# A hybrid decoder step (Conformer convolution and mLSTM) on one core: the head loop's norm, tile sums, state output and the place of the weight splits reordered

## The chip, the cores and the metric

The kernel runs on one core of one Trainium2 chip. The metric is the time of one execution on the device, in microseconds (us). A core has TensorE (PE in the rows, with its weight load as PEld), VectorE (DVE), ScalarE (ACT), GpSimd (POOL) and SyncE (SP). They run side by side and wait for each other through semaphores.

## The reference

One trunk layer runs over 512 prompt tokens and over 8 decode sequences of 4 tokens. Cut to what matters here, the mLSTM branch, for each of 4 heads with DK = 256 and DV = 512:

```python
s = jnp.einsum('bthk,bshk->btsh', qc, kc) * w_intra
num = jnp.einsum('btsh,bshv->bthv', s, vc) + w_inter[..., None] * jnp.einsum('bhvk,bthk->bthv', C, qc)
den = jnp.sum(s, axis=2) + w_inter * jnp.einsum('bhk,bthk->bth', n, qc)
h = num / jnp.maximum(jnp.abs(den), jnp.exp(-m_t))[..., None]
C_new = dec[..., None, None] * C + jnp.einsum('bsh,bshv,bshk->bhvk', wk, vc, kc)
n_new = dec[..., None] * n + jnp.einsum('bsh,bshk->bhk', wk, kc)
...
hm = hm * lax.rsqrt(jnp.mean(hm * hm, axis=-1, keepdims=True) + EPS) * g_mh.reshape(M_HEADS, DV)
hm = hm.reshape(B, T, D_M).astype(x.dtype) * jax.nn.sigmoid(o)
y_m = jnp.einsum('btm,md->btd', hm, w_m_out)
```

With N = num and d = max(|den|, exp(-m)), N/d normed is N / sqrt(mean(N^2) + EPS d^2). Around this branch stand the input projection, a 31-tap depthwise convolution, gates, an output projection and a two-matrix MLP. All tensors are float32.

## The kernel before

Every weight is streamed from memory in chunks of 128 output features (512 KB). SyncE loads a chunk into one of two buffers `wraw`, ScalarE copies it as rounded float into `whi` (a ring of 4), VectorE writes the rest `wlo = wraw - whi`, and TensorE makes each product from three partial ones (whi with ahi, whi with alo, wlo with ahi). The function `hi` issues the ScalarE part, `lo` the VectorE part; inside the head loop both are called by `split(k)`, where k counts the head's 12 chunks: 0 to 3 are q and k, 4 to 7 are v, 8 to 11 are the output gates o0 to o3. `split(12)`, `split(13)` and `split(14)` already belong to the next head's q0, q1 and k0. SyncE refills a `wraw` buffer when the `lo` of it is done.

The order of the work is written out by hand for each engine, and an engine takes its list in that order. The head loop (`with pe.Fori(0, HEADS)` and the same on the others) is run 4 times. TensorE has two product buffers in PSUM, slot 0 and slot 1. The table `USES` lists what a head puts into them: an even place is slot 0, an odd one slot 1. TensorE may write a use only when the use before it in the same slot has been drained (`use(name)` waits for `drained`). Its o chunks are in slots 0, 1, 0, 1. Between them it makes the outer products cu0 to cu7 (`outer(n)`, new terms of the decode sequences' matrix memories), each of which is drained by VectorE's `update(n)` of the ring `crg` (L1145). `readout(i)` multiplies four of the old memories with the queries. After o3 come the weighted values pv0 to pv3 (`weighted(k)`), and the prompt's new memory (`new_state(half)`), which uses the slots as cc01 and cc23.

In the o section ScalarE and VectorE run this (before):

```python
# ScalarE                                    # VectorE
split(10)                                    rden = max(rden, exp(-m)); taps(15, 16); split(10)
for k in range(VT):                          for k in range(VT):
    split(11 + k)                                if k != 1: taps(*O_TAPS[k])
    hm_k = sigmoid(product of o_k)               split(11 + k)
                                                 if k == 1: taps(*O_TAPS[k])
                                                 if k < 2: update(2 * k); update(2 * k + 1)
```

`taps(a, b)` (L1035) runs taps a to b-1 of the depthwise convolution, two instructions a tap; they need nothing of the products and are spread over the head as filling. In the pv section VectorE multiplies each pv by the reciprocal `rden` into `hr` (L1168), multiplies the gate `hm` by that (L1171), and adds the squares that ScalarE makes of `hr` into `sqacc` (L1176). A matmul with ones sums them over partitions, and ScalarE makes the root. `den` is a matmul of ones with the four tiles of `pt`; the normaliser sums are eight one-column matmuls over `kw`.

Of the kernel before, what the change touches and what calls it, by code (L numbers as in the profile page):

```python
# [11 lines left out]
P = 128  # L12
# [37 lines left out]
        "cu4", "pv0", "cu5", "pv1", "cc01", "cu6", "pv2", "cu7", "pv3", "cc23"]  # L50
# [42 lines left out]
DVE_PER_HEAD = 81  # L93
# [22 lines left out]
def hybrid_layer(nc, xT, wstream, w_gates, cols, b_gates, b_v, w_dw, hist, c_in, n_in, m_in,  # L116
# [8 lines left out]
    with ctx:  # L125
# [30 lines left out]
        eps = at("eps", [P, 1], f32)  # L156
        warm = at("warm", [P, 1], f32)
# [41 lines left out]
        bv = at("bv", [P, DV], f32, cursor[0])  # L199
        hr = at("hr", [P, 2, SEQ], f32)  # L200
# [98 lines left out]
        np_ready, np_used, nn_ready = sem("np_ready"), sem("np_used"), sem("nn_ready")  # L299
# [102 lines left out]
        def _(pool):  # L402
# [28 lines left out]
            pool.memset(sel[:, :], 0.0).then_inc(pool_step, 1)  # L431
            for j in range(QUAD):
                pool.wait_ge(pool_step, 18 + j)
                pool.affine_select(out=sel[:, :], in_=sel[:, :], compare_op=ALU.not_equal, fill=1.0, base=-NS * j,
                                   pattern=[[-1, NS]], channel_multiplier=1).then_inc(pool_step, 1)
# [52 lines left out]
            def prompt_state(h):  # L488
                for name in ("cc01", "cc23"):
                    wait_drained(pool, h, name)  # L490
# [14 lines left out]
            with pool.Fori(0, HEADS - 1) as h:  # L505
# [8 lines left out]
                pool.wait_ge(head_done, h + 1)  # L514
# [14 lines left out]
        def _(act):  # L529
# [98 lines left out]
            act.wait_ge(pool_step, 22)  # L628
            with act.Fori(0, HEADS) as h:
# [88 lines left out]
                def state_out(half):  # L718
                    s = use(("cc01", "cc23")[half])
                    act.activation(cst[:, 2 * half:2 * half + 2, :].rearrange("p a k -> p (a k)"), psum[s][:, 0, :],  # L720
                                   ACT.Copy).then_inc(drained[s], 1)

                act.wait_ge(np_ready, h + 1)
                act.activation(npn[:, bass.ds(h, 1), :], side[:, 2:3, P:P + QT], ACT.Copy).then_inc(np_used, 1)
                for k in range(VT):
                    was_drained(f"pv{k}")
                    if k == 3:
                        act.wait_ge(hsum_ready, 3 * h + 1)
                    dst = sqacc[:, :] if k == 0 else sqh[:, k % 2, :]
                    act.activation(dst, hr[:, k % 2, :], ACT.Square).then_inc(hsq_ready, 1)  # L730
                    if k == 1:
                        state_out(0)
# [3 lines left out]
                act.activation(sqacc[:, :], side[:, 1, :], ACT.Ln, bias=eps[:, :], scale=1.0 / DV).then_inc(var_ready, 1)  # L736
# [124 lines left out]
        def _(dve):  # L861
# [148 lines left out]
            dve.wait_ge(pool_step, 22)  # L1010
            with dve.Fori(0, HEADS) as h:
# [88 lines left out]
                for s_ in range(ST):  # L1100
# [5 lines left out]
                    if s_ >= 2:  # L1106
                        if s_ == 3:
                            dve.wait_ge(dve_step, sums_at)
                        n = sample_products(s_ - 2)
                    if s_ < 3:  # L1110
# [25 lines left out]
                rd = mark(V.tensor_tensor(rden[:, :], rden[:, :], hb[:, R_M:R_M + SEQ], ALU.max))  # L1136
                dve.wait_ge(sden_abs, h + 1)
                sd = mark(V.tensor_tensor(sst[:, 0:1], sst[:, 0:1], mcol[:, hh], ALU.max))
                taps(15, 16)
# [8 lines left out]
                for k in range(VT):  # L1148
                    if k != 1:
                        taps(*O_TAPS[k])  # L1150
                    split(11 + k)
                    if k == 1:
                        taps(*O_TAPS[k])
# [3 lines left out]
                    if k == 1:  # L1157
                        dve.wait_ge(dve_step, sd)
                        V.reciprocal(sst[:, 1:2], sst[:, 0:1]).then_inc(srec_ready, 1)
                        dve.wait_ge(dve_step, rd)  # L1160
                        rd = mark(V.reciprocal(rden[:, :], rden[:, :]))
                dve.wait_ge(dve_step, rd)
                for k in range(VT):
                    update(4 + k)
                    s = use(f"pv{k}")
                    if k >= 2:
                        dve.wait_ge(hsq_ready, VT * h + (k - 1))
                    V.tensor_tensor(hr[:, k % 2, :], psum[s][:, 0, :], rden[:, :], ALU.mult).then_inc(drained[s], 1)  # L1168
                    was_drained(f"pv{k}")
                    d = tile(hm, 4 * h + k, 0, SEQ)  # L1170
                    n = mark(V.tensor_tensor(d, d, hr[:, k % 2:k % 2 + 1, :], ALU.mult))  # L1171
                    if k >= 1:
                        dve.wait_ge(hsq_ready, VT * h + (k + 1))
                        if k >= 2:
                            dve.wait_ge(hsum_ready, 3 * h + (k - 1))
                        V.tensor_tensor(sqacc[:, :], sqacc[:, :], sqh[:, k % 2, :], ALU.add).then_inc(hsum_ready, 1)  # L1176
                    taps(*PV_TAPS[k])
                taps(26, WIDTH - 1)
# [8 lines left out]
                dve.wait_ge(dve_step, n)  # L1187
# [578 lines left out]
```

## Time and profile before

| | us |
|---|---|
| median of 3 runs (lowest, highest) | 1281.4 (1280.85, 1281.85) |
| profiled execution, its own time | 1282.05 |
| its span in the trace | 1280.4 |
| TensorE busy | 1242.6 |
| VectorE busy | 730.1 |
| ScalarE busy | 494.2 |

The profiled execution's own time is 1.65 us above its span and 0.65 us above the median. TensorE's busy time is the union of its matmuls' times. The mean granted TensorE clock of the span is 0.988 of full speed.

### The profile page before, as it was taken

The numbers are of one execution on the slowest core, as the hardware profiler recorded it, in microseconds if no ns is written. First come the engines' busy times: TensorE is split into PE (matmuls) and PEld (weight loads), VectorE is DVE, ScalarE is ACT, GpSimd is POOL, SyncE is SP. The second block draws the span as 40 slices with busy tenths as digits, with TensorE's granted clock in tenths as the row PEclk, the third lists the DMA queues.
The fourth block names the chain that finished last, engine by engine and source line by source line (L and its number), as shares of the span: only waits on it lengthen the run. The fifth ranks groups of instructions, "written<-read, shape, count | busy, mean of one in ns | idle before, by whom it ended". The sixth has DMA issues, their size and how long they took to land.

```text
span 1280.4 us, 23631 instructions
## 1 busy us (share of the span) xinstructions
PE 1242.6 (97%) x9079; PEld 1164.1 (91%) x9079; DVE 730.1 (57%) x984; ACT 494.2 (39%) x738; POOL 68.6 (5%) x130
## 2 busy tenths in 40 slices
PE   7999999999999999999999999998999999999994
PEld 6999978888797888879999999997999999999993
DVE  6342688888878888888455433337453213443324
ACT  5333543343354335335543222236564223543211
POOL 3010001101100110010000000000000000000002
PEclk8999999999999999999999999998999999999997
DMA  6235216515441641442322222430323222223211
GB/s 205 81 117 186 83 66 214 187 37 186 172 145 41 221 178 62 150 162 84 100 82 99 83 90 78 149 99 34 104 94 99 82 98 82 83 82 99 82 49 70
DMA packets 39328, 141.29 MB, mean 110 GB/s; under 512 B 4788, under 2 KB 5172, under 8 KB 39144
## 3 DMA queue, kind: packets, MB, share of 16 engines
q1 hardware_dynamic: 27848, 99.37, 23.2%
q0 software_dynamic: 11424, 41.23, 9.1%
q8 instruction: 29, 0.48, 0.1%
q14 instruction: 27, 0.22, 0.1%
HBM read 118.31 MB, written 22.26 MB: 110 GB/s over the span
## 4 chain that ended last, share of the span: by engine, by line
PE 91%; DVE 4%; issue 2%; ACT 2%; DMA 1%; DVEq 0%; POOLq 0%; POOL 0%; SPq 0%; ACTq 0%
PE product L1365 85%; PE side L1365 6%; DVE hr L1168 1%; DVE hm L1191 1%; DVE accp L1035 1%; DMA x<-in_xT 1%; DVE y L1279 1%; DVE crg L1145 0%; ACT sqh L730 0%; ACT L700 0%; PE side L1523 0%; DVE qT L1056 0%; ACT rst L551 0%; DVE hm L1184 0%; ACT rst L553 0%
## 5 line engine op out<-in xcount | busy, mean ns | idle before, releaser
L872 DVE TENSOR_TENSOR wlo<-wraw,whi 128x1024 fp32r<-128x1024 f32 x176 | 215.3, 1224 | 234.6 <-ACT whi L535 220.8
L1365 PE MATMUL product<-ahi,whi 128*128 128x256 f32 x1520 | 319.4, 291 | 12.1 <-DVE alo L1289 5.9
L1365 PE MATMUL product<-ahi,wlo 128*128 128x256 f32 x1520 | 315.3, 289 | 0.0
L1365 PE MATMUL product<-alo,whi 128*128 128x256 f32 x1520 | 313.5, 287 | 0.0
L535 ACT ACTIVATE whi<-wraw 128x1024 fp32r<-128x1024 f32 x176 | 184.3, 1052 | 237.1 <-PE product L1365 183.9
L1365 PEld LDWEIGHTS product<-ahi,whi 128*128 128x128 f32 x1520 | 244.9, 190 | 19.6 <-issue 11.9
L1365 PEld LDWEIGHTS product<-alo,whi 128*128 128x128 f32 x1520 | 244.4, 189 | 0.0
L1365 PEld LDWEIGHTS product<-ahi,wlo 128*128 128x128 f32 x1520 | 243.7, 189 | 0.0
L1035 DVE SCALAR_TENSOR_TENSOR accp<-u,wdw,accp 128x512 f32<-128x512 f32 x240 | 162.9, 742 | 0.3
L1365 PE MATMUL product<-hidhi,wlo 128*128 128x256 f32 (+1 forms) x512 | 105.8, 287 | 0.0
L1365 PE MATMUL product<-hidlo,whi 128*128 128x256 f32 (+1 forms) x512 | 105.7, 288 | 0.0
L1365 PE MATMUL product<-hidhi,whi 128*128 128x256 f32 (+1 forms) x512 | 104.8, 286 | 0.0
L1365 PEld LDWEIGHTS product<-hidhi,wlo 128*128 128x128 f32 x512 | 82.0, 188 | 0.0
L1365 PEld LDWEIGHTS product<-hidhi,whi 128*128 128x128 f32 x512 | 81.9, 188 | 0.0
L1365 PEld LDWEIGHTS product<-hidlo,whi 128*128 128x128 f32 x512 | 81.2, 188 | 0.0
L1314 DVE TENSOR_TENSOR hidlo<-fr,hidhi 128x544 f32 (+1 forms) x32 | 23.2, 726 | 74.9 <-ACT hidhi L822 74.9
L1365 PE MATMUL product<-whi,ahi 128*128 128x512 f32 (+1 forms) x160 | 56.4, 352 | 0.0
L1365 PE MATMUL product<-wlo,ahi 128*128 128x512 f32 (+1 forms) x160 | 55.6, 347 | 0.0
L1365 PE MATMUL product<-whi,alo 128*128 128x512 f32 (+1 forms) x160 | 55.4, 346 | 0.0
L1365 PE MATMUL product<-mhi,wlo 128*128 128x256 f32 (+1 forms) x256 | 52.9, 288 | 0.0
L1365 PE MATMUL product<-bhi,wlo 128*128 128x256 f32 (+1 forms) x256 | 52.9, 288 | 0.0
L1365 PE MATMUL product<-mhi,whi 128*128 128x256 f32 (+1 forms) x256 | 52.9, 288 | 0.0
(268 smaller groups left out, 1604.7 us busy)
## 6 DMA issues: line engine op xcount, KB each, us to landing
wraw<-in_wstream SPq DMA_DIRECT2D x176, 512.0 KB, 3.3
crg<-in_c_in POOLq DMA_DIRECT2D x32, 512.0 KB, 5.9
out_c_s<-crg POOLq DMA_DIRECT2D x32, 512.0 KB, 2.9
hb<-head_rows POOLq DMA_DIRECT2D x4, 580.0 KB, 5.5
x<-in_xT SPq DMA_DIRECT2D x4, 544.0 KB, 5.7
sgm<-in_xT SPq DMA_DIRECT2D x1, 2176.0 KB, 9.0
out_yT<-y SPq DMA_DIRECT2D x8, 272.0 KB, 2.1
out_c_p<-cst POOLq DMA_DIRECT2D x4, 512.0 KB, 8.5
```

Source lines behind the costliest of these rows:

```text
L535: act.activation(whi[:, k % RING, :, :], wraw[:, k % 2, :, :], ACT.Copy).then_inc(hi_done, 1)
L872: V.tensor_tensor(wlo[:, k % RING, :, :], wraw[:, k % 2, :, :], whi[:, k % RING, :, :].bitcast(f32), ALU.subtract).then_inc(lo_done, 1)
L1035: ins = V.scalar_tensor_tensor(sum_, src, w, sum_, ALU.mult, ALU.add)
L1168: V.tensor_tensor(hr[:, k % 2, :], psum[s][:, 0, :], rden[:, :], ALU.mult).then_inc(drained[s], 1)
L1191: ins = V.scalar_tensor_tensor(d, d, c("g_mh", 4 * h + k), sqacc[:, :].rearrange("p (a t) -> p a t", a=1), ALU.mult, ALU.mult)
L1279: V.scalar_tensor_tensor(tile(y, j), tile(y, j), c(gain, j), rst3, ALU.mult, ALU.mult).then_inc(y_scaled, 1)
L1314: V.tensor_tensor(tile(hidlo, j), fr[:, 2 + b:3 + b, :], tile(hidhi, j).bitcast(f32), ALU.subtract).then_inc(hid_lo, 1)
L1365: return pe.matmul(out, lhsT, rhs, start=start, stop=stop, skip_group_check=check)
```

## The change

- `USES` loses cc01 and cc23. The new state is made in four quarters in the PSUM tensor `side`, a quarter ahead of each weighted value, the last one in two halves around pv3. ScalarE copies it from there; new semaphores `cc_ready` and `cst_ready` stand for the slots' ones.
- The denominator no longer divides: d squared, scaled, is the first term of `sqacc`, and the norm's root is taken of the whole. The reciprocal of `rden` (L1161) and the products `hr` (L1168) are gone; ScalarE squares pv straight from PSUM and VectorE multiplies the gate by pv.
- VectorE adds the tiles of `pt` into `sqacc` and those of `kw` into the new tile `ksum`, so that the ones-matmuls for the denominator are two instead of four and those for the normaliser two instead of eight.
- `readout(0)` comes ahead of o0 on TensorE, and the one-column matmuls come behind `outer(2)`.
- On ScalarE the load of the sigmoid's table (the `warm` activation) comes ahead of the loop over the o chunks, and in the loop the sigmoid of o_k now comes ahead of `split(11 + k)`. On VectorE `split(11 + k)` comes first for every k, and the taps are dealt out anew. GpSimd's load of the next head's bias no longer waits for `head_done`.

The core of the diff:

```diff
-V_TAPS = [(5, 8), (8, 11), (11, 15)]
-O_TAPS = [(16, 17), (17, 19), (19, 23), (23, 24)]
-PV_TAPS = [(24, 24), (24, 26), (26, 26), (26, 26)]
+V_TAPS = [(5, 8), (8, 11), (11, 14)]
+O_TAPS = [(14, 14), (14, 17), (17, 22), (22, 24)]
+PV_TAPS = [(24, 25), (25, 26), (26, 27), (27, 27)]
...
                 act.activation(rden[:, :], side[:, 0, :], ACT.Abs).then_inc(den_abs, 1)
-                act.wait_ge(sden_ready, h + 1)
-                act.activation(sst[:, 0:1], side[:, 2, 0:1], ACT.Abs).then_inc(sden_abs, 1)
                 split(10)
+                act.wait_ge(d_ready, h + 1)
+                act.activation(sqacc[:, :], rden[:, :], ACT.Square, scale=(EPS * DV / P) ** 0.5).then_inc(hsq_ready, 1)
+                act.activation(warm[:, :], eps[:, :], ACT.Sigmoid).then_inc(table_in, 1)
                 for k in range(VT):
-                    split(11 + k)
-                    if k == 0:
-                        act.activation(warm[:, :], eps[:, :], ACT.Sigmoid).then_inc(table_in, 1)
                     s = use(f"o{k}")
                     act.activation(tile(hm, 4 * h + k), slot(s), ACT.Sigmoid, bias=c("b_o", 4 * h + k)).then_inc(drained[s], 1)
+                    split(11 + k)
+                    if k == 1:
+                        act.wait_ge(sden_ready, h + 1)
+                        act.activation(sst[:, 0:1], side[:, 2, 0:1], ACT.Abs).then_inc(sden_abs, 1)
+                        act.activation(npn[:, bass.ds(h, 1), :], side[:, 2:3, P:P + QT], ACT.Copy).then_inc(np_used, 1)
...
                 for k in range(VT):
-                    if k != 1:
-                        taps(*O_TAPS[k])
                     split(11 + k)
-                    if k == 1:
-                        taps(*O_TAPS[k])
+                    taps(*O_TAPS[k])
                     if k < 2:
                         update(2 * k)
                         update(2 * k + 1)
...
-                    V.tensor_tensor(hr[:, k % 2, :], psum[s][:, 0, :], rden[:, :], ALU.mult).then_inc(drained[s], 1)
-                    was_drained(f"pv{k}")
+                    dve.wait_ge(hsq_ready, (VT + 1) * h + (k + 2))
                     d = tile(hm, 4 * h + k, 0, SEQ)
-                    n = mark(V.tensor_tensor(d, d, hr[:, k % 2:k % 2 + 1, :], ALU.mult))
+                    if k < VT - 1:
+                        V.tensor_tensor(d, d, psum[s][:, 0:1, :], ALU.mult).then_inc(drained[s], 1)
                     if k >= 1:
+                        dve.wait_ge(hsum_ready, VT * h + k)
+                    V.tensor_tensor(sqacc[:, :], sqacc[:, :], sqh[:, k % 2, :], ALU.add).then_inc(hsum_ready, 1)
...
+                pe.wait_ge(wsum_ready, h + 1)
+                mm(side[:, 0, 0:P], ones[:, :], pt[:, 0:P], True, True)
+                mm(side[:, 0, P:SEQ], ones[:, :], sqacc[:, P:SEQ], True, True).then_inc(den_ready, 1)
+                readout(0)
+                chunk("o0", 8)
...
+                for k in range(VT):
+                    outer(4 + k)
+                    if k == VT - 1:
+                        new_state(k, range(2))
+                    elif k > 0:
+                        new_state(k)
+                    weighted(k)
+                new_state(VT - 1, range(2, ST))
```

**The order on ScalarE, around the sigmoid of o1.** `hm` is the gate, product0 and product1 are the slots, `whi` is the `hi` step of a split. Before, from the sigmoid of o0 on:

```order
L702 ACTIVATE hm_73<-product0,col_52 128x544
L532 REGISTER_ALU
L535 ACTIVATE whi_50<-wraw_49 128x1024 [waits chunk_done,raw_in0]
L321 REGISTER_ALU
L702 ISA [waits chunk_done]
L702 REGISTER_ALU
L702 ACTIVATE hm_73<-product1,col_52 128x544
```

Now, from the same place on:

```order
L703 ACTIVATE hm_74<-product0,col_52 128x544
L537 REGISTER_ALU [waits raw_in1]
L538 ACTIVATE whi_50<-wraw_49 128x1024 [waits chunk_done]
L325 REGISTER_ALU
L703 ISA [waits chunk_done]
L703 REGISTER_ALU
L703 ACTIVATE hm_74<-product1,col_52 128x544
L535 REGISTER_ALU
L538 ACTIVATE whi_50<-wraw_49 128x1024 [waits chunk_done,raw_in0]
```

The copy of chunk 12 (the one with raw_in0) stood ahead of o1's sigmoid and its wait for the end of chunk o1 and now stands behind them; between the two sigmoids there is now that of chunk 11.

**The order on VectorE, around update(2).** `crg` is an update of a matrix memory, `wlo` the `lo` step of a split, `accp` a tap. Before, from update(1) on:

```order
L1145 SCALAR_TENSOR_TENSOR crg_116<-crg_116,hb_93,product0 128x1024 [waits ready0]
...
L872 TENSOR_TENSOR wlo_51<-wraw_49,whi_50 128x1024 [waits hi_done]
...
L1035 SCALAR_TENSOR_TENSOR accp_113<-u_82,wdw_53,accp_113 128x512
...
L1145 SCALAR_TENSOR_TENSOR crg_116<-crg_116,hb_93,product0 128x1024 [waits ready0]
L1145 SCALAR_TENSOR_TENSOR crg_116<-crg_116,hb_93,product1 128x1024 [waits ready1]
```

Now:

```order
L1159 SCALAR_TENSOR_TENSOR crg_117<-crg_117,hb_94,product0 128x1024 [waits ready0]
...
L875 TENSOR_TENSOR wlo_51<-wraw_49,whi_50 128x1024 [waits hi_done]
...
L1038 SCALAR_TENSOR_TENSOR accp_114<-u_83,wdw_53,accp_114 128x512
...
L1159 SCALAR_TENSOR_TENSOR crg_117<-crg_117,hb_94,product0 128x1024 [waits ready0]
L1159 SCALAR_TENSOR_TENSOR crg_117<-crg_117,hb_94,product1 128x1024 [waits ready1]
```

The sequence is the same, but the row of the tap stands for 4 instructions before and for 6 now, and the `wlo` is in both that of chunk 12, whose `hi` has moved on ScalarE.

**The order on TensorE, around o2.** `product0<-vst,kst` is the outer product cu2, `product1<-vst,kst` is cu3, and the last row is the first matmul of o2. Now:

```order
L1373 MATMUL product0<-vst_112,kst_111 128x512 [waits drained0]
...
L1373 MATMUL side<-ones_54,ksum_97 128x1 [waits ksum_ready]
...
L1373 MATMUL product1<-vst_112,kst_111 128x512 [waits drained1]
...
L1373 MATMUL product0<-ahi_71,whi_50 128x256 [waits drained0]
```

o2 takes slot 0 behind cu2, as before; between cu2 and cu3 stand now five one-column matmuls (two of `ksum`, one of `pts`, two of `qn`) where eight of `kw` stood.

## Rows read from the trace of the kernel before

**Rows 1.** The page: busy us (share of the span) xinstructions of two engines.

```profile
PE 1242.6 (97%) x9079; PEld 1164.1 (91%) x9079; DVE 730.1 (57%) x984; ACT 494.2 (39%) x738; POOL 68.6 (5%) x130
```

**Rows 2.** Waits of PE over the whole span: us in total, times, longest.

```profile
PE product L1365 <- DVE hr L1168: 2.6, 8, 0.3
...
PE product L1365 <- DVE qT L1056: 2.1, 3, 0.8
```

**Rows 3.** Timeline of PE, third head: start us, us, instruction [idle before <-releaser].

```profile
404.93 2.32 PE L1365 MATMUL side<-pt,ones 128*128 128x512 f32 x8
...
414.12 1.92 PE L1365 MATMUL side<-crg,qm 128*32 128x512 f32 x16
...
417.48 1.12 PE L1365 MATMUL side<-vtok,pts 32*128 32x512 f32 x2
418.53 0.52 PE L1365 MATMUL product<-ahi,whi 128*128 128x256 f32 x2
...
424.63 0.62 PE L1365 MATMUL product<-vst,kst 96*128 96x512 f32 x2
425.10 1.84 PE L1365 MATMUL side<-ones,kw 128*128 128x1 f32 x16
426.80 0.71 PE L1365 MATMUL product<-vst,kst 96*128 96x512 f32 x2
427.35 0.42 PE L1365 MATMUL product<-ahi,whi 128*128 128x256 f32 x2
...
439.42 1.92 PE L1365 MATMUL side<-crg,qm 128*32 128x512 f32 x16
...
443.92 0.70 PE L1365 MATMUL product<-vst,kst 96*128 96x512 f32 x2
...
447.21 3.62 PE L1365 MATMUL product<-kw,vtok 128*128 128x256 f32 x16
...
461.37 1.02 PE L1365 MATMUL side<-sqacc,ones 128*128 128x512 f32 x2
```

**Rows 4.** Timeline of DVE in the same stretch, same columns.

```profile
416.75 2.47 DVE L1145 SCALAR_TENSOR_TENSOR crg<-crg,hb,product 128x1024 f32<-128x1024 f32 x2 [0.34 <-PE product L1365]
419.13 1.22 DVE L872 TENSOR_TENSOR wlo<-wraw,whi 128x1024 fp32r<-128x1024 f32 x1
420.27 2.74 DVE L1035 SCALAR_TENSOR_TENSOR accp<-u,wdw,accp 128x512 f32<-128x512 f32 x4
425.30 1.28 DVE L1145 SCALAR_TENSOR_TENSOR crg<-crg,hb,product 128x1024 f32<-128x1024 f32 x1 [2.29 <-PE product L1365]
...
459.83 6.71 DVE L1035 SCALAR_TENSOR_TENSOR accp<-u,wdw,accp 128x512 f32<-128x512 f32 x10
```

**Rows 5.** Timeline of ACT in the same stretch, same columns.

```profile
413.59 1.06 ACT L535 ACTIVATE whi<-wraw 128x1024 fp32r<-128x1024 f32 x1 [1.55 <-DMA wraw<-in_wstream]
414.67 1.28 ACT L700 ACT_TABLE_LOAD   x1
...
417.31 1.06 ACT L535 ACTIVATE whi<-wraw 128x1024 fp32r<-128x1024 f32 x1 [0.54 <-DMA wraw<-in_wstream]
425.05 0.71 ACT L702 ACTIVATE hm<-product,col 128x544 f32 x1 [6.68 <-PE product L1365]
425.66 1.05 ACT L535 ACTIVATE whi<-wraw 128x1024 fp32r<-128x1024 f32 x1
```

**Rows 6.** Timeline of PE after its longest idle time, in the MLP; same columns.

```profile
873.60 0.79 PE L1365 MATMUL product<-ahi,whi 128*128 128x256 f32 x2 [5.93 <-DVE alo L1289]
...
878.20 0.41 PE L1365 MATMUL product<-alo,whi 128*128 128x256 f32 x2
```

**Rows 7.** Windows there: stretch, length, busy of PE PEld DVE ACT POOL, PEclk, DMA.

```profile
870.00:872.00 2.00, 0.00 (x0) 0.00 (x0) 1.97 (x3) 0.60 (x1) 0.00 (x0) 0.82 0.00 0
...
876.00:878.00 2.00, 2.00 (x10) 2.00 (x10) 1.96 (x4) 1.21 (x3) 0.00 (x0) 0.50 0.00 0
878.00:880.00 2.00, 2.00 (x18) 2.00 (x17) 1.97 (x4) 1.03 (x2) 0.00 (x0) 0.98 0.00 0
```

More of the change, by code:

```diff
@@ L49 @@
         "o0", "cu0", "cu1", "o1", "cu2", "cu3", "o2", "o3",
-        "cu4", "pv0", "cu5", "pv1", "cc01", "cu6", "pv2", "cu7", "pv3", "cc23"]
+        "cu4", "pv0", "cu5", "pv1", "cu6", "pv2", "cu7", "pv3"]
 USES_HEAD = len(USES) // 2
@@ L1135, in _ @@
                 dve.wait_ge(expm_ready, h + 1)
[L1136 to L1139, printed above, removed]
+                V.scalar_tensor_tensor(rden[:, :], hb[:, R_M:R_M + SEQ], D_CAP, rden[:, :], ALU.min, ALU.max).then_inc(d_ready, 1)
                 split(10)
@@ L1565, in weighted, with new_state @@
                     ins.then_inc(ready[s], 1)
-                def new_state(half):
-                    s = use(("cc01", "cc23")[half])
-                    for r in range(2):
-                        for q in range(ST):
-                            v = P * (2 * half + r)
-                            ins = mm(psum[s][:, 0, DK * r:DK * (r + 1)], vtok[:, q, v:v + P], kw[:, q, :], q == 0, q == ST - 1)
-                    ins.then_inc(ready[s], 1)
-                pe.wait_ge(pt_ready, 5 * h + 5)
-                for q in range(ST):
-                    ins = mm(side[:, 0, P * q:SEQ], ones[:, :], pt[:, PT_AT[q]:PT_AT[q] + SEQ - P * q], q == 0, q == ST - 1)
-                ins.then_inc(den_ready, 1)
-                pe.wait_ge(ops_ready, 5 * h + 4)
+                def new_state(v, tiles=range(ST)):
+                    half, r = divmod(v, 2)
+                    for q in tiles:
+                        ins = mm(side[:, half, DK * r:DK * (r + 1)], vtok[:, q, P * v:P * (v + 1)], kw[:, q, :], q == 0, q == ST - 1)
+                    if r == 1 and q == ST - 1:
+                        ins.then_inc(cc_ready, 1)
+                pe.wait_ge(pt_ready, 5 * h + 5)
+                pe.wait_ge(wsum_ready, h + 1)
[3 more added lines that the diff above has]
+                chunk("o0", 8)
+                pe.wait_ge(ops_ready, 5 * h + 5)
+                pe.wait_ge(vs_all, h + 1)
+                pe.wait_ge(kst_ready, 3 * DEC_B * (h + 1))
+                outer(0)
+                mm(side[:, 3, :], pts[:, :], vtok[0:NS, ST, :], False, False)
+                outer(1)
+                chunk("o1", 9)
+                outer(2)
+                pe.wait_ge(ksum_ready, h + 1)
+                for kk in range(QT):
+                    mm(side[:, 2, P + kk:P + kk + 1], ksum[:, P * kk:P * (kk + 1)], ones[:, 0:1], True, True)
                 mm(side[:, 2, 0:1], pts[:, :], ones[0:NS, 0:1], True, False)
@@ L1584, in _ @@
                 ins.then_inc(sden_ready, 1)
-                chunk("o0", 8)
-                readout(0)
-                pe.wait_ge(ops_ready, 5 * h + 5)
-                pe.wait_ge(vs_all, h + 1)
-                pe.wait_ge(kst_ready, 3 * DEC_B * (h + 1))
-                outer(0)
-                outer(1)
-                mm(side[:, 3, :], pts[:, :], vtok[0:NS, ST, :], False, False)
-                chunk("o1", 9)
-                outer(2)
-                pe.wait_ge(sden_abs, h + 1)
-                for kk in range(QT):
-                    for q in range(ST):
-                        ins = mm(side[:, 2, P + kk:P + kk + 1], kw[:, q, P * kk:P * (kk + 1)], ones[:, 0:1], q == 0, q == ST - 1)
-                ins.then_inc(np_ready, 1)
                 outer(3)
```

92 lines of the change are left out of this document (47 added, 45 removed).

## The prediction, made blind

> **What bounds the kernel now.** I read the page first: TensorE is busy for 1242.6 us of the span, VectorE for 730.1 and ScalarE for 494.2 [rows 1]. So the time is TensorE's list plus its gaps, and an edit elsewhere counts when it opens or closes one. The waits of TensorE in the head loop are small: 2.6 us in 8 waits for the products `hr`, and 2.1 us in 3 waits for `qT` at the start of a head [rows 2]. Then I read the timelines of the three engines over one head. The rows to look at are the ones around o1 and o2: VectorE does update(0) 0.34 us after it could, waiting for TensorE, and it stood idle 2.29 us before update(2), for TensorE again [rows 4]. So before, VectorE is ahead of TensorE by about 2 us where o2 needs its slot. ScalarE copies chunk 12 at 417.31, over 7 us ahead of o1's sigmoid at 425.05, and chunk 13 right behind that sigmoid [rows 5]. That lead is what the change touches. All times below are those of the third head; the others have the same list.
>
> **What TensorE saves.** The four ones-matmuls for the denominator take 2.25 us from start to next (the row at 404.93, 8 records for 1280 columns) [rows 3]; two matmuls of 512 columns in all take 512/1280 of it, 0.90: 1.35 us saved. The eight one-column matmuls over `kw` take 1.70 (425.10 to 426.80), two take 0.43: 1.27 saved. Matmuls of the new state are the same in number. Together 2.6 us a head, 10.5 in all. With the waits for `hr` gone (2.6) the best case of the change is 13 us.
>
> **VectorE's added and removed work** counts only through the order. Three additions of `kw` (256 wide) and three of `pt` (384, 256, 128 wide) replace a tap and the reciprocal; the `pt` sums stand behind v3, while TensorE makes v4, and I cost their wait at nothing (the cover is v4's own product; if it were missing, the sums' own length of under 1.5 us a head would be the price, by twice the 0.67 us of a tap [rows 4]).
>
> **Step A, o1.** o0 now starts at 404.93 + 0.90 + 1.9 (the readout's row at 414.12) = 407.7, and ends 6.1 later (418.53 to 424.63) at 413.8. TensorE then has cu0 0.47, the product of `pts` 1.05 and cu1 0.47 [rows 3] and wants o1 at 415.8. o1 needs slot 1, so update(0). VectorE now has `split(11)` ahead of it, and ScalarE has o0's sigmoid ahead of that. A sigmoid starts 0.42 after TensorE's next row (424.63 to 425.05), the copy follows 0.61 later and takes 1.05 [rows 5], the `wlo` takes 1.14, the update 1.28 [rows 4]; with 0.1 for two handovers the slot is free at 413.8 + 4.6 = 418.4. Before, o1 began at 418.53. So TensorE waits 2.6 us, and the 1.35 saved ahead of it and the one-column matmuls that moved away are gone into that wait: gain 0.1.
>
> **Step B, o2.** This is the large one. Counted from the end of o1 (424.5): sigmoid +0.42, copy of chunk 12 +0.61 and 1.05, `wlo` 1.14, six taps at 0.67 = 4.0 (ten take 6.71, four 2.74), update(2) 1.28, handovers 0.1: o2 starts 8.6 us after o1's end, at 433.1. Before it was 427.35 [rows 3], since chunk 12 was split long ago and the taps done. TensorE's own list in between is cu2 0.47, five one-column matmuls 1.2 and cu3 0.55, so it stands still for about 6.4 us. Price: 5.8 us a head.
>
> **Step C, the clock.** Such a pause was in the trace once: 5.93 us idle, in the course of which the granted clock fell (0.82 in one stretch of 2 us, 0.50 afterwards, 0.98 again in the last) [rows 7], that is from 2.4 to 1.2 GHz, and the ten pairs of matmuls behind it took 4.6 us, 873.60 to 878.20 [rows 6], where ten pairs take 2.5 at full clock (a chunk has 48 matmuls, 24 pairs, in its 6.1). I take the same 2.1 us for each of the four pauses; the bounds are 0 and, with the smaller pauses of step A and D also bringing it down, three times that.
>
> **Step D, o3 and the pv section.** o3 follows o2 at once. TensorE's list reaches the point of the old `readout(1)` at 433.1 + 2.1 + 12.07 (427.35 to 439.42) = 447.3. VectorE: o2 ends at 441.3; sigmoid, copy and `wlo` as above bring it to 444.6, ten taps to 451.3, `split(14)` to 452.4, four taps to 455.1, update(4) to 456.4. TensorE would want the slot (cu5) after a quarter of the new state, 1.8 (half of the row at 447.21), and after readout, cu4 and pv0, 4.5 (439.42 to 443.92), at 453.6. A wait of 2.8. From there the list is that of 443.92 to 461.37, 17.45 us, less 1.4 of old waits (three, 0.3 to 0.4 in the row and some 0.15 at the issue) and less the quarter that now lies ahead, 1.8, plus some 0.5 for updates that come just late: 14.8. The matmul for the sum of squares is at 471.2 instead of 461.37: **+9.8 us a head**, of which B is 5.8 (A's gain in it), C 2.1 and D 1.9. For the four heads 39.2.
>
> **Step E, the next head.** k0 waits for `qT`, 0.7 us each time [rows 2]. Before, VectorE's last ten taps end at 459.83 + 6.7 = 466.5, 5.1 after the start of the sum's matmul at 461.37 [rows 3, 4]. Now the last addition ends just ahead of that matmul, and a product (0.67, the length of a tap of the same width) and eight taps (5.4) follow: 6.0. The list behind is the same, so this wait grows by 0.8, three times: 2.4.
>
> Edits that I cost at nothing: the earlier table load (1.28 us [rows 5]; it stands while TensorE is in o0, where ScalarE is idle; cost 1.28 a head if o0 were over), the new squares and copies (the same number as before within one), GpSimd's bias load (no one waits for it in these rows), and the earlier `readout(0)` (its memories are loaded while the q to v chunks run).
>
> **Sum.** 1282.05 (the profiled execution's own time) + 39.2 + 2.4 = 1323.65; less the 0.65 by which that execution lies above the median: **1323.0 us**.
>
> **The rivals.** *The clock holds.* The waits of under 3 us in A and D do nothing to it and the fall behind o2's pause doesn't come: 8.4 less, 1314.6. Against it speaks that an idle time of the same length was followed by 1.2 GHz [rows 6, 7]. *It falls in three places a head.* After 2.6 to 2.8 us of idle time in front of o1 and cu5 as well: up to 2.1 more each, 8 times, 1340; some of that would lie in waits that are there anyway, so between the two. For it speaks that a pause is closely followed by the next. Against it, 0.3 us waits leave no mark in the head loop, and there is no row with a pause of this length.
>
> The Trainium skill, in TensorE: Matmul & The Clock Gate, section "A second HAM failure mode: psum-queue depth-cycling", describes a kernel in which many short idle times between groups of matmuls kept the clock swinging between half and full rate. By that rule the result would be this second rival's. The trace's short waits do not bear it out so far, and the longest one agrees only in what a long pause does.
>
> *The waits do not come and it is faster.* The mechanism: update(2) is done within the 2.2 us that TensorE has between o1 and o2, so the saved matmuls reach the end. Then 2.6 a head and the waits for `hr` come off: 1281.4 - 13 = 1268.4. It decides at a length of 2.2 us for the chain behind o1's sigmoid, and mine is 8.6; only if copy and `wlo` of chunk 12 ran ahead of the sigmoid, which the orders of both engines exclude, or VectorE did not take its list in order, would it be near. For it speaks only that VectorE had 2.29 us to spare at this point. *The change does not do what it says* in one way: a part of the pause is recovered (VectorE, idle in between, arrives earlier in the pv section than I count). That gives 1300 to 1312.
>
> **How the numbers follow.** My forecast as it stands, with the clock's loss in one place: 0.60, 1316 to 1330. The clock holds: 0.11. Three places: 0.15. Partly recovered: 0.07. Faster: 0.03. Two or three terms cancel to the old time: 0.01; slower beyond 1340: 0.03. For 8 in 10 the range must take in the forecast, the held clock and most of the three places: 1312 to 1337. A measurement of this kernel can tell 0.2%, 2.6 us, from no change. Faster 0.03, same 0.01, slower 0.96.
>
> **What would show it.** In the profile after: TensorE idle for about 6.4 us before o2's first matmul with the VectorE update as its releaser, four times; before it six taps, a `wlo`, a copy and o1's sigmoid without a gap; a granted clock of 0.5 in o2's first microseconds; waits of 2.6 before o1 and 2.8 before cu5. Fewer matmul records of `ones`. VectorE idle 6 to 7 us ahead of the `wlo` of chunks 12 and 13. The prediction is wrong if o2 starts less than 5 us after o1's end, or if the chain of waits shows no sigmoid of the gate in front of the splits.

## The result, and the profile after

The changed kernel takes 1336.5 us (median of 4 runs, 1334.0 to 1336.9), against 1281.5: a ratio of 1.0426 (95% interval 1.0408 to 1.0444), slower by 55 us. The prediction had the direction, the mechanism and the range (1312 to 1337) right; its number, 1323.0, is 13.5 us short. The range holds by 0.5 us only, and with some luck: one term was wrong in the other direction (step E below).

The busy line of the page [rows 1], and the waits of TensorE [rows 2], after:

```profile
PE 1258.5 (94%) x9015; PEld 1182.0 (89%) x9015; DVE 717.1 (54%) x992; ACT 494.9 (37%) x742; POOL 68.6 (5%) x131
```

```profile
PE product L1373 <- DVE crg L1159: 45.5, 16, 6.5
```

TensorE has 64 matmuls fewer, and is busy 15.9 us longer, since some stretches ran at half clock (below). The waits for `hr` and `qT` are gone, as forecast for the first only. In their place stand 16 waits for an update of `crg`, 45.5 us: in each head those before o1, o2 and cu5, and one of 0.3 before cu7. The profiled execution takes 1336.9 us with a span of 1335.2, and its mean granted clock is 0.964 (0.988 before).

TensorE in the third head, as [rows 3]: start us, us, instruction, [idle before <-releaser].

```profile
429.86 0.38 PE L1373 MATMUL side<-pt,ones 128*128 128x128 f32 x2
...
430.82 1.92 PE L1373 MATMUL side<-crg,qm 128*32 128x512 f32 x16
...
443.52 0.79 PE L1373 MATMUL product<-ahi,whi 128*128 128x256 f32 x2 [2.37 <-DVE crg L1159]
...
452.31 0.63 PE L1373 MATMUL product<-vst,kst 96*128 96x512 f32 x2
452.78 0.50 PE L1373 MATMUL side<-ones,ksum 128*128 128x1 f32 x4
...
453.99 0.70 PE L1373 MATMUL product<-vst,kst 96*128 96x512 f32 x2
460.95 0.82 PE L1373 MATMUL product<-ahi,whi 128*128 128x256 f32 x2 [6.26 <-DVE crg L1159]
...
475.64 1.89 PE L1373 MATMUL side<-kw,vtok 128*128 128x256 f32 x8
...
484.59 0.73 PE L1373 MATMUL product<-vst,kst 96*128 96x512 f32 x2 [2.39 <-DVE crg L1159]
...
499.19 1.13 PE L1373 MATMUL side<-sqacc,ones 128*128 128x512 f32 x2
```

Set beside [rows 3], this splits the head's 69.3 us (429.86 to 499.19; 56.4 before) into stretches that can be set beside the steps of the forecast:

| stretch | before | after | difference | forecast |
|---|---|---|---|---|
| denominator to o1 | 13.60 | 13.66 | +0.1 | -0.1 |
| o1 to cu2 | 6.10 | 8.79 | +2.7 | 0 |
| cu2 to o2 | 2.72 | 8.64 | +5.9 | +5.9 |
| o2 and o3 | 12.07 | 14.69 | +2.6 | +2.1 |
| to the sum of squares | 21.95 | 23.55 | +1.6 | +1.9 |
| sum | 56.44 | 69.33 | +12.9 | +9.8 |

VectorE in the same stretch, as [rows 4]:

```profile
440.83 1.23 DVE L875 TENSOR_TENSOR wlo<-wraw,whi 128x1024 fp32r<-128x1024 f32 x1 [2.64 <-ACT whi L538]
442.09 2.47 DVE L1159 SCALAR_TENSOR_TENSOR crg<-crg,hb,product 128x1024 f32<-128x1024 f32 x2
454.50 1.23 DVE L875 TENSOR_TENSOR wlo<-wraw,whi 128x1024 fp32r<-128x1024 f32 x1 [9.94 <-ACT whi L538]
455.65 4.06 DVE L1038 SCALAR_TENSOR_TENSOR accp<-u,wdw,accp 128x512 f32<-128x512 f32 x6
459.62 2.47 DVE L1159 SCALAR_TENSOR_TENSOR crg<-crg,hb,product 128x1024 f32<-128x1024 f32 x2
```

ScalarE there, as [rows 5]:

```profile
437.47 1.28 ACT L700 ACT_TABLE_LOAD   x1
...
439.14 0.71 ACT L703 ACTIVATE hm<-product,col 128x544 f32 x1 [0.17 <-PE product L1373]
439.75 1.05 ACT L538 ACTIVATE whi<-wraw 128x1024 fp32r<-128x1024 f32 x1
452.81 0.71 ACT L703 ACTIVATE hm<-product,col 128x544 f32 x1 [12.01 <-PE product L1373]
453.43 1.05 ACT L538 ACTIVATE whi<-wraw 128x1024 fp32r<-128x1024 f32 x1
```

The chain of step B reads straight off: o1 ends at 452.31, sigmoid 452.81, copy 453.43, `wlo` 454.50, six taps 455.65, update(2) 459.62, o2 460.95. VectorE had stood idle for 9.94 us ahead of that `wlo`, with the taps in hand and the update behind them.

The granted clock in windows of that head (stretch, length, busy of PE PEld DVE ACT POOL, then PEclk, DMA share, GB/s, as [rows 7]):

```profile
442.00:444.00 2.00, 0.48 (x2) 0.51 (x3) 1.97 (x3) 0.00 (x0) 0.00 (x0) 0.68 0.40 82
444.00:446.00 2.00, 2.00 (x11) 2.00 (x10) 0.56 (x1) 0.00 (x0) 1.09 (x2) 0.50 0.85 338
...
452.00:456.00 4.00, 2.69 (x18) 2.15 (x17) 1.50 (x2) 1.78 (x4) 0.00 (x0) 1.00 0.00 0
456.00:460.00 4.00, 0.00 (x0) 0.00 (x0) 4.00 (x7) 0.00 (x0) 0.00 (x0) 0.55 0.39 131
...
462.00:464.00 2.00, 2.00 (x10) 2.00 (x10) 0.32 (x3) 0.00 (x0) 1.19 (x3) 0.50 0.66 262
...
484.00:488.00 4.00, 3.41 (x13) 2.57 (x14) 4.00 (x6) 0.00 (x0) 0.54 (x1) 1.00 0.32 131
```

It is down to 1.2 GHz (0.50) in o1 and again in o2, and at full speed after the wait before cu5 (484:488). All four heads show this, so eight falls. From o1 to cu2 the four heads take 8.6 to 8.8 us, o2 and o3 14.5 to 14.7, where the kernel before has 6.1 and 12.1: 20.8 us more in all.

### The profile page after: what moved, and what is told of

Read it like the earlier page. It is cut to its first block, busy times and chain, and to the rows that moved or that the text cites. A ratio compares the mean times of both kernels' runs of the same rounds, so it can differ in the third digit from the quotient of the medians.

```text
span 1335.2 us, 23473 instructions
## 1 busy us (share of the span) xinstructions
PE 1258.5 (94%) x9015; PEld 1182.0 (89%) x9015; DVE 717.1 (54%) x992; ACT 494.9 (37%) x742; POOL 68.6 (5%) x131
## 4 chain that ended last, share of the span: by engine, by line
PE 87%; DVE 6%; issue 4%; ACT 2%; DVEq 1%; DMA 1%; ACTq 0%; POOLq 0%; POOL 0%; SPq 0%
PE product L1373 81%; PE side L1373 5%; DVE accp L1038 2%; DVE crg L1159 1%; ACT whi L538 1%; DMA x<-in_xT 1%; DVE y L1287 0%; DVE wlo L875 0%; PE side L1531 0%; DVE alo L900 0%; DVEq L1037 0%; DVE fr L892 0%; DVE sqacc L1182 0%; DVEq L1038 0%; ACT sqh L733 0%
## 5 line engine op out<-in xcount | busy, mean ns | idle before, releaser
L1373 PE MATMUL product<-ahi,whi 128*128 128x256 f32 x1520 | 328.2, 298 | 45.0 <-DVE crg L1159 34.7
L1373 PE MATMUL product<-ahi,wlo 128*128 128x256 f32 x1520 | 323.2, 295 | 0.0
L1373 PE MATMUL product<-alo,whi 128*128 128x256 f32 x1520 | 322.9, 295 | 0.0
L1373 PEld LDWEIGHTS product<-ahi,whi 128*128 128x128 f32 x1520 | 255.6, 196 | 55.4 <-DVE crg L1159 26.9
L1373 PEld LDWEIGHTS product<-alo,whi 128*128 128x128 f32 x1520 | 254.6, 196 | 0.0
L1373 PEld LDWEIGHTS product<-ahi,wlo 128*128 128x128 f32 x1520 | 252.7, 195 | 0.0
L703 ACT ACTIVATE hm<-product,col 128x544 f32 x16 | 11.4, 715 | 127.8 <-PE product L1373 127.8
L1373 PE MATMUL product<-blo,whi 128*128 128x256 f32 (+1 forms) x256 | 53.1, 288 | 0.0
```

The costliest lines, as they stand in the source:

```text
L1373: return pe.matmul(out, lhsT, rhs, start=start, stop=stop, skip_group_check=check)
```

## The experiments

The question was what the 55 us consist of, and what of the change is worth keeping. Diffs are against the kernel named ahead of each.

**1. The split ahead of the sigmoid again, on ScalarE alone** (against the changed kernel):

```diff
                 for k in range(VT):
+                    split(11 + k)
                     s = use(f"o{k}")
                     act.activation(tile(hm, 4 * h + k), slot(s), ACT.Sigmoid, ...).then_inc(drained[s], 1)
-                    split(11 + k)
```

> The changed kernel with one thing put back: in the loop over the output chunks ScalarE makes split(11 + k) ahead of the sigmoid again. Theory (the copy behind the sigmoid makes update(0), update(2) and update(4) late, and TensorE's clock falls in the pauses): the pauses before o1, o2 and cu5 go, and the clock stays at 2.4 GHz in the head loop; 1266 to 1276 us, below the kernel before. Rival (the new pv section and the sums on VectorE cost it): 1310 or more, since only the order on ScalarE differs.

Measured: 1283.2 us, ratio to the kernel before 1.0012 (1.0000 to 1.0025). One call in ScalarE's list is worth 53 of the 55 us. But the gain that I expected beyond it (1266 to 1276) is not there. The four starts of o1 in its trace show the reason:

```profile
190.45 0.49 PE L1373 MATMUL product<-ahi,whi 128*128 128x256 f32 x2 [1.33 <-DVE crg L1159]
301.96 0.79 PE L1373 MATMUL product<-ahi,whi 128*128 128x256 f32 x2 [1.33 <-DVE crg L1159]
414.60 0.80 PE L1373 MATMUL product<-ahi,whi 128*128 128x256 f32 x2 [1.33 <-DVE crg L1159]
527.34 0.79 PE L1373 MATMUL product<-ahi,whi 128*128 128x256 f32 x2 [1.33 <-DVE crg L1159]
```

The same 1.33 us stop is there four times, and in three of them the first pair of matmuls takes 0.79 instead of 0.49: half clock. The four stops make 5.3 us. From o1 to cu2 it takes 6.10 us in the first head, at full clock, and 7.37, 7.37 and 8.86 in the others: 5.3 more. Without the two it would be about 1273, as expected. In the chain that ends the stop ScalarE has the 1.28 us table load ahead of chunk 11's copy, and VectorE has chunk 11's `wlo` ahead of update(0).

**2. The sigmoid ahead of the split, in the kernel before** (against it; the same call moved the other way):

```diff
                 for k in range(VT):
-                    split(11 + k)
                     ...
                     act.activation(tile(hm, 4 * h + k), slot(s), ACT.Sigmoid, ...).then_inc(drained[s], 1)
+                    split(11 + k)
```

> The kernel before with one thing changed: the sigmoid of o_k ahead of split(11 + k) on ScalarE. Theory: four taps instead of six stand in the chain behind o1's end, which is then 7.3 us long against 2.7 of TensorE's own work, so o2 comes 4.6 us later a head, and the clock falls once a head for 2.6 us more: 1306 to 1314 us. Rival (the taps' new places matter, not the sigmoid): under 1290.

Measured: 1310.4 us, ratio 1.0224 (1.0207 to 1.0241), inside the expectation. Waits of TensorE:

```profile
PE product L1365 <- DVE crg L1145: 21.5, 12, 4.6
```

o2 came 7.3 us after o1's end, as expected. The clock fell in o2 in each head and, beyond the expectation, once in o1 (first head, behind a stop of 0.91; the stops of 0.53 there in the other heads left no fall). Alone the order costs 29 us; with the rest of the change it costs 53. The rest brings TensorE to o2 earlier and puts two more tap instructions ahead of update(2), so the stop is longer (6.3 for 4.4), it lengthens the stop before o1 (2.4 for 0.5 to 0.9), and it adds the one before cu5.

**3. The stops filled with work** (against the changed kernel; ones times ones into a bank that nobody reads then):

```diff
                 outer(1)
+                for _ in range(9):
+                    mm(side[:, 1, 0:P], ones[:, :], ones[:, :], True, True)
                 chunk("o1", 9)
...
                 outer(3)
+                for _ in range(25):
+                    mm(side[:, 1, 0:P], ones[:, :], ones[:, :], True, True)
                 chunk("o2", 10)
```

> The changed kernel with matmuls of ones by ones (128 columns, result not used) in TensorE's pauses: 9 before o1 (2.0 us) and 25 before o2 (5.5 us). They end before the slot is free. If the fall of the clock is 2.6 us at each of the eight places, it is 21 us faster than the changed kernel, 1315 us, with a granted clock of 1.0 in o1 and o2. If the pauses alone cost the time: 1336 or a little more.

Measured: 1323.0 us, ratio 1.0329 (1.0312 to 1.0347): 13.4 less instead of 21. o1 and o2 did run at full clock. First head: their starts, and cu5's; second head: cu5's.

```profile
192.13 0.49 PE L1373 MATMUL product<-ahi,whi 128*128 128x256 f32 x2 [0.37 <-DVE crg L1159]
207.06 0.52 PE L1373 MATMUL product<-ahi,whi 128*128 128x256 f32 x2 [0.87 <-DVE crg L1159]
228.16 0.73 PE L1373 MATMUL product<-vst,kst 96*128 96x512 f32 x2 [2.39 <-DVE crg L1159]
...
349.16 0.74 PE L1373 MATMUL product<-vst,kst 96*128 96x512 f32 x2 [2.39 <-DVE crg L1159]
```

The windows behind the last row show what took the rest back:

```profile
349.00:351.00 2.00, 1.84 (x6) 1.55 (x7) 2.00 (x5) 0.00 (x0) 0.54 (x1) 0.76 0.07 29
351.00:353.00 2.00, 2.00 (x6) 1.55 (x6) 1.83 (x2) 0.00 (x0) 0.00 (x0) 0.50 0.58 234
```

The clock now fell behind the 2.39 us stop before cu5, in three of four heads. The same stop left it alone in the changed kernel and in this run's first head. The first head, with no fall at all, is 4.9 us shorter than in the changed kernel, the others 3.4 to 3.6; the fall behind cu5 costs them 1.7 (from cu5 to cu6 6.07 us for 4.37). So the falls at o1 and o2 cost at least 13 us, and whether a fall follows a stop of this length is not settled by the length.

**4. No shift of the buffers** (against the changed kernel). Its new one-column tensor `tiny` lies between the small tensors and moves every later buffer in the on-chip memory by 32 bytes. Here it shares the 32 bytes of `eps`:

```diff
-        eps = at("eps", [P, 1], f32)
-        tiny = at("tiny", [P, 1], f32)
+        small = at("eps", [P, 8], f32)
+        eps, tiny = small[:, 0:1], small[:, 4:5]
```

> The changed kernel with the constant tiny in the same 32 bytes as eps, so that the operands ahi, alo, hm and all behind them lie at the addresses of the kernel before (as far as the removed and added tiles allow). Theory (the dense matmuls of the changed kernel run 0.5% slower, 801 in 100 us against 807, because their operands moved by 32 bytes): 807 again, and about 6 us less, 1330. Rival (it is the run or the chip): 1336 and no difference in rate to the changed kernel.

Measured: 1326.8 us, ratio 1.0354 (1.0336 to 1.0371): 9.7 less, where 6 were expected. The rate is back: in a stretch in which TensorE is never idle 403 matmuls fit into 50 us (the changed kernel's row stands below, with 400).

```profile
700.00:750.00 50.00, 50.00 (x403) 50.00 (x402) 27.69 (x34) 21.15 (x30) 0.00 (x0) 1.00 0.26 89
```

From the last head's sum of squares to the end it took 705.2 us, where the changed kernel takes 709.7 and the kernel before 705.1. By the spans of the profiled executions (1328.1 for 1335.2) the gain is 7.1, and 6.0 of it lie outside the heads. Inside the heads the clock also went otherwise: it fell nine times, once behind a stop of 2.43 us before cu5 (second head), and stayed low for a shorter time in two o1 (from o1 to cu2 7.33 and 7.59 us for 8.73 and 8.79). So about 6 us belong to the shift, and what is beyond may be the clock's.

**5. and 6. The kernel before, shifted by 32 bytes, and by 64** (against it; `[P, 1]`, then `[P, 16]`):

```diff
         eps = at("eps", [P, 1], f32)
+        pad = at("pad", [P, 1], f32)
```

> The kernel before with 32 bytes of unused space ahead of the constant warm, so that the operands ahi, alo, hm and all behind them move by 32 bytes, and nothing else. If the place of the operands sets the rate of the dense matmuls: about 401 records in 50 us of the output section where the kernel before has 403, 321 in 40 us of the first section instead of 323, and 5 to 7 us more, 1287. If the rate belongs to the run: 1281.5.

> The same with 64 bytes instead of 32. If it is the place within 64 bytes that counts: 1281.5 and the rate of the kernel before. If any move costs: 1287.

Measured: 1288.6 us by 32 bytes, ratio 1.0045 (1.0028 to 1.0061); 1283.8 by 64, ratio 1.0012 (1.0002 to 1.0022). A stretch in which TensorE is never idle gives the rate again. In the kernel before, then in the changed one, then shifted by 32, then by 64:

```profile
700.00:750.00 50.00, 50.00 (x403) 50.00 (x402) 21.79 (x27) 13.00 (x17) 0.00 (x0) 1.00 0.26 85
```

```profile
700.00:750.00 50.00, 50.00 (x400) 50.00 (x400) 26.48 (x33) 22.07 (x31) 0.00 (x0) 1.00 0.28 90
```

```profile
700.00:750.00 50.00, 50.00 (x401) 50.00 (x399) 21.64 (x26) 13.42 (x17) 0.00 (x0) 1.00 0.27 90
```

```profile
700.00:750.00 50.00, 50.00 (x403) 50.00 (x402) 20.69 (x24) 13.41 (x17) 0.00 (x0) 1.00 0.29 94
```

At full clock and 50.00 us busy, 403 matmuls fit, or 400 and 401 after a shift by 32. Half a per cent is little, and over 1280 us it would be 6; from the last sum of squares to the end it is 2.7 (707.8 us for 705.1), and 0.6 by 64. That 64 bytes do no such harm and 32 do speaks for the placement, and against the added tensor as such. In both runs the clock also fell in two heads of four, each time in o2, where the kernel before has no fall (0.66 in 200 to 205 and 316 to 321 by 32; 0.57 in 428 to 432 and 544 to 548 by 64), so some of the two differences is the clock's: the heads with a fall take 1.5 to 1.8 us more (58.2 by 32, 58.0 by 64, for 56.4). And it fell there without a stop. By 64 bytes, third head, TensorE's timeline:

```profile
425.94 1.84 PE L1366 MATMUL side<-ones,kw 128*128 128x1 f32 x16
427.64 0.71 PE L1366 MATMUL product<-vst,kst 96*128 96x512 f32 x2
...
428.52 0.66 PE L1366 MATMUL product<-alo,whi 128*128 128x256 f32 x2
```

A pair that takes 0.41 at full clock takes 0.66 here, with no idle time shown ahead of it. What lies ahead is the sixteen records of one column each: TensorE is busy by its records and does little work. But the same records stand ahead of o2 in every head of the kernel before, where the clock doesn't fall, so they alone don't decide it.

**7. The six tap instructions behind update(2) and update(3)** (against the changed kernel):

```diff
-                    taps(*O_TAPS[k])
+                    if k != 1:
+                        taps(*O_TAPS[k])
                     if k < 2:
                         update(2 * k)
                         update(2 * k + 1)
                     if k == 1:
+                        taps(*O_TAPS[k])
```

> The changed kernel with the six taps between the wlo of chunk 12 and update(2) put behind update(3). By the chain behind o1's end the slot is free after 4.6 us instead of 8.6 and the pause before o2 falls from 6.3 to 2.3 us: 16 us less, 1320, where the clock still falls in that pause as it does before o1, and 1310 where it no longer does. If the taps do not stand in the chain: 1336.

Measured: 1318.4 us, ratio 1.0278 (1.0261 to 1.0295), 18 less, near the 16 expected. The taps are in the chain: the stop before o2 is 4.0 us shorter in each head. But the heads gain 2.5, 6.2, 3.8 and 6.4, not 4.0 each, since the falls, again two a head, last a shorter time in the second and fourth (from o1 to cu2 7.4 us for 8.8), and o1 came 0.9 later in the first. That the sum comes out so near is in part luck. In its second head o2 waits 2.29 us now (6.26 before this edit); the stops at o1 and cu5 are the same:

```profile
314.84 0.79 PE L1375 MATMUL product<-ahi,whi 128*128 128x256 f32 x2 [2.37 <-DVE crg L1159]
...
326.93 0.52 PE L1375 MATMUL product<-ahi,whi 128*128 128x256 f32 x2 [2.29 <-DVE crg L1159]
```

**8. The mended version** (against the changed kernel): experiments 1 and 4 together, and update(0) and update(1) ahead of chunk 11's `wlo`; two tap instructions moved from the pv section to o3.

```diff
-O_TAPS = [(14, 14), (14, 17), (17, 22), (22, 24)]
-PV_TAPS = [(24, 25), (25, 26), (26, 27), (27, 27)]
+O_TAPS = [(14, 14), (14, 17), (17, 22), (22, 25)]
+PV_TAPS = [(25, 25), (25, 26), (26, 27), (27, 27)]
...
                 for k in range(VT):
+                    if k == 0:
+                        update(0)
+                        update(1)
                     split(11 + k)
                     taps(*O_TAPS[k])
-                    if k < 2:
-                        update(2 * k)
-                        update(2 * k + 1)
+                    if k == 1:
+                        update(2)
+                        update(3)
```

> The changed kernel with the constant tiny beside eps (no shift), split(11 + k) ahead of the sigmoid on ScalarE, update(0) and update(1) ahead of split(11) on VectorE, and one tap moved from behind pv0 to the third stretch of o taps. The waits before o1, o2 and cu5 and the falls of the clock go, the saved matmuls stay: 1260 to 1268 us, faster than both. Rival (the new section is itself longer): 1275 or more.

Measured: 1271.1 us, ratio 0.9909 (0.9893 to 0.9926): ahead of both kernels, 3 us above the range I expected. o2 still waits for six taps and update(2), once `readout(1)` waits for its memories, and twice in the loop (first and third head) the clock fell in o2:

```profile
308.32 0.52 PE L1376 MATMUL product<-ahi,whi 128*128 128x256 f32 x2 [0.59 <-DVE crg L1159]
...
323.23 1.06 PE L1376 MATMUL side<-crg,qm 128*32 128x512 f32 x8 [0.94 <-DMA crg<-in_c_in]
```

```profile
198.00:202.00 4.00, 4.00 (x22) 4.00 (x21) 3.97 (x8) 0.00 (x0) 1.54 (x4) 0.57 0.76 186
420.00:424.00 4.00, 4.00 (x22) 4.00 (x21) 3.96 (x8) 0.00 (x0) 1.93 (x4) 0.58 0.70 176
```

**9. One tap less ahead of update(2)** (against the mended version):

```diff
-O_TAPS = [(14, 14), (14, 17), (17, 22), (22, 25)]
+O_TAPS = [(14, 14), (14, 16), (16, 22), (22, 25)]
```

> The mended version with one tap (two instructions, 1.35 us of VectorE) moved from ahead of update(2) to ahead of the split of chunk 13. In the mended version o2 waits 0.59 us for update(2) in every head. Expected: that wait is gone, 4 x 0.6 = 2.4 us less, 1268.7. Rival: the wait moves to another buffer, because chunk 13's and 14's splits and the pv section come later by as much; then the time stays at 1271.1. Where the clock falls differs from run to run of a kernel's variants, so 2 us either way are open.

Measured: 1264.2 us, ratio 0.9861 (0.9844 to 0.9877): the best of all, 17.4 below the kernel before. The step was 6.9 us, not 2.4. o2's wait is gone, and with it both falls and the wait of `readout(1)`:

```profile
PE product L1376 <- ACT hm L704: 1.4, 3, 1.0
...
PE product L1376 <- DVE crg L1159: 1.2, 4, 0.3
```

```profile
170.00:340.00 170.00, 168.22 (x1050) 139.20 (x1049) 140.92 (x210) 68.38 (x118) 17.46 (x33) 1.00 0.43 151
340.00:560.00 220.00, 219.10 (x1394) 185.70 (x1393) 184.49 (x290) 95.72 (x174) 21.95 (x40) 1.00 0.41 149
```

TensorE stands idle for 2.7 us of these 390, nearly the whole head loop, at full clock throughout. Head by head the gain over experiment 8 is 1.6, 1.8, 2.4 and 0.8 us. The fourth, with no fall in either, shows what the wait is worth; a fall adds 1.6 in the third, and the transfer's 0.9 lies in the second. In the first head cu1 waits 1.0 us for o0's sigmoid, which stands behind the table load (the wait for `hm` above). That the falls went because the wait went fits, and isn't proved: experiments 5 and 6 have falls at o2 with no wait, so the one-column matmuls ahead of it may be enough in some heads. Nor is it shown that the missing transfer wait has to do with the edit. Each program's own runs agree closely (1263.5 to 1264.5 here, 1270.6 to 1271.8 in experiment 8).

**10. The kernel before with two taps fewer**, to explain why the waits for `qT` went:

```diff
-PV_TAPS = [(24, 24), (24, 26), (26, 26), (26, 26)]
+PV_TAPS = [(24, 24), (24, 24), (26, 26), (26, 26)]
```

> The kernel before without taps 24 and 25 of the depthwise convolution (both tiles, in every head; the output lacks them). It makes the list that VectorE repeats per head shorter (about 333 instructions instead of 345; the changed kernel has 339), and it takes 2.7 us of work from a part of the list in which VectorE is ahead of TensorE. Theory: the 3.4 us in which VectorE waited for nothing the profile shows, at the start of heads two to four, come from the length of the repeated list, and they are why TensorE waited 0.7 us for qT three times. Then both are gone here, the 27 packets of VectorE's instruction queue are about 12 as in the changed kernel, and the time is 1279 to 1280. Rival: the gap hangs on something else in the order (the reciprocal, the divided taps); then it stays at 3.4 us three times, with 27 packets; the qT waits may still vanish, since VectorE is 2.7 us ahead. Rival 2: nothing changes, 1281.4.

Measured: 1279.1 us, ratio 0.9981 (0.9971 to 0.9990). In the trace of the kernel before VectorE shows this among its waits, and the page this packet count (queue, kind: packets, MB, share). That q14 is VectorE's is read only from how its count goes with VectorE's gap:

```profile
DVE wlo L872 <- issue: 9.8, 3, 3.4
...
q14 instruction: 27, 0.22, 0.1%
```

Here the first is absent, the waits for `qT` are too, and the page has

```profile
q14 instruction: 12, 0.10, 0.0%
```

The changed kernel also has 12 and no such wait; all four versions of the kernel before with the full list have 27 and three gaps. The waits of TensorE for `hr` and `crg` are those of the kernel before, so the theory on the list holds, and the rival (VectorE merely being further ahead) would have left the 27. The instruction counts are the expectation's, about 345, 339 and 333; whether it is the length that counts or where the list ends isn't separated.

## Why the prediction was right, and where it was not

- **What TensorE saves**, 2.6 us a head, is real, but in the changed kernel it lies wholly in stops. With the orders mended it comes out: the second head takes 52.4 us in experiment 9 (286.49 to 338.91) instead of 56.5, 4.1 less. The waits for `hr` are 0.65 of the rest; what is left was not taken apart.
- **Step A** right: a wait of 2.37 for the forecast 2.6.
- **Step B** right: o2 started 8.64 us after o1's end, forecast 8.6, and the wait was 6.26 for 6.4. Experiments 1, 2 and 7 show the links that an edit can move: the split behind the sigmoid, and the taps ahead of the update. One sign was off: VectorE stood idle for 9.9 and 9.4 us ahead of the `wlo` of chunks 12 and 13, for the forecast 6 to 7.
- **Step C** failed as put: "I take the same 2.1 us for each of the four pauses". The clock fell twice a head, after o1's stop of 2.4 us too, and a fall cost 2.4 to 2.7 us of chunk time. That is 20.8 us in all for the forecast 8.4, 12.4 more and nearly the whole miss: both the number of falls and the price of one were too small. The rival with three places named the mechanism; of its places the one before cu5 did not fall. Of the Trainium skill's page TensorE: Matmul & The Clock Gate, section "A second HAM failure mode: psum-queue depth-cycling", the trace now agrees that short stops between groups of matmuls can swing the clock: eight falls in the changed kernel, and experiment 3 is 13 us shorter with two stops a head filled. My argument against it, that stops of 0.3 us left no mark, said nothing of stops of 2.4.
- **Step D** right within 0.3: 1.6 for 1.9, cu5's wait 2.39 for 2.8.
- **Step E** wrong in sign. The stretch from the sum of squares to the next denominator is 56.9 us for 57.4 to 57.6 before. VectorE's tail is as late as I counted, but I took the wait for `qT` as the tail's doing. Its cause was VectorE's 3.4 us gap at the end of its repeated list, and experiment 10 shows that gap to hang on the list. -1.7 for +2.4: without this error the forecast would have been 4.1 us further off.
- **Not in the sum at all:** the shift by 32 bytes. Between the changed kernel and experiment 4 it is 9.7 us by the medians and 7.1 by the spans, 6.0 of it outside the heads and 4.5 of that behind the last one.
- **Rightly at nothing:** the table load. In the third head it ends (437.47 + 1.28) just ahead of o0's end, 438.80. In experiment 9's first head o0 was over by then, and the wait behind the load was 1.0 us.

The account against the spans: the four heads +51.4, the stretches between them -1.7, ahead of the first head +0.5, behind the last +4.6 (709.7 for 705.1). Together 54.8, as measured (1335.2 - 1280.4). Against my 41.6 (39.2 and 2.4) that leaves +12.2, -4.1, +0.5 and +4.6.

The rival "faster" named the one thing that decides: the copy and the `wlo` of chunk 12 running ahead of the sigmoid. It put 1268.4 on it. Experiment 1 shows that this alone is not enough (1283.2), and experiments 8 and 9, with the other stops and the shift gone, reach 1271.1 and 1264.2.

**What stays open.** Why a stop of 2.4 us before cu5 brings the clock down in three heads of experiment 3, in one of experiment 4 and in none of the changed kernel, why a fall costs 1.3 us in one head and 2.8 in the next behind the same stop (experiments 1 and 7), and why it falls at o2 in two heads of four, behind a stop of 0.59 (experiment 8) and behind none (5 and 6). So the clock's part in a difference of 2 to 5 us between two versions can't be foretold from their stops; in the changed kernel, with the same two falls in each of four heads, it can be read. These counts of falls are from one profiled execution of each kernel. What exactly in the placement by 32 bytes slows the matmuls is open too; which operand is at fault was not tried.

## What to carry to other kernels

Before an operation that waits for a product (an activation that drains it) is put ahead of a weight split, follow what is queued behind it on every engine: here one swapped pair on ScalarE held up a copy, a `wlo`, six taps and an update, each in another engine's way, 8.6 us where TensorE had 2.2 of its own. Price a stop of TensorE with the clock's fall behind it, also for stops of 1 to 3 us, and then remove the stops to the last: taking away the last 0.6 us a head gave 6.9 us, not 2.4, as two falls and a wait for a transfer went too. Fillers such as the taps belong behind the operation that frees a buffer, and a new small tensor where it moves no large one.

## What the runs showed of the hardware

- **The granted clock** fell to 1.2 GHz in o1 or o2 behind stops of 6.3, 4.4, 2.4 and 1.3 us, once behind 0.9 (experiment 2) and, in two heads of four, behind 0.6 or no stop at all but one-column matmuls. It did not fall behind some stops of 2.4 (before cu5) and 1.33 (first head of experiment 1). A fall cost 2.4 to 2.7 us in the changed kernel, and 1.3 to 2.8 over all versions, of a chunk that otherwise takes 6.1. With matmuls in the stops it stayed up in o1 and o2 (experiment 3), and in three heads it fell behind the stop before cu5 instead.
- **32 bytes** of shift cost the dense matmul stretches half a per cent (400 or 401 for 403 in 50 us); 64 bytes cost no rate (403).
- **A loop's list** mattered on VectorE: with about 345 instructions in the repeated list 3.4 us of idle time without a releaser at each of three returns and 27 packets in q14; with about 339, or 333, none and 12. The Trainium skill's page Advanced Engine Details and Errata, section "ISA Cache", gives an engine's store of instructions as two lines of 256. Two such lines would hold 512 instructions, more than any of these lists, so that figure alone doesn't explain the step; no run shows which lines a list touches. The runs show the step between about 339 and 345 instructions, for these lists.
